# A decoder kernel without its filler transposes of the identity on TensorE

## The chip, the cores and the metric

The kernel runs on one core of one Trainium2 chip. The metric is device time in microseconds (us) of one execution; the values given are medians over runs. Lower is better. TensorE (PE in the profile) does the matrix products, ScalarE (ACT) and VectorE (DVE) the elementwise work and the copies out of the PSUM banks, GpSimd (POOL) some elementwise work, and SyncE (SP) issues the weight transfers. The profile gives TensorE's granted clock as a share of full speed: 1.00 is 2.4 GHz and 0.50 is 1.2 GHz, its two levels.

## The reference

A sequence of 256 rows of width 1024 goes through one block of one kind and four layers of another, in float32:

```python
x = x + 0.5 * _swiglu(_rmsnorm(x, n1_g[l]), ffn1_w_in[l], ffn1_w_out[l])      # d_ff 2816
h = _rmsnorm(x, n2_g[l])
qa, ka, va, qb, kb, vb, qi, ki, wi, ga, gb = jnp.split(h @ w_in[l], split_points, axis=-1)
o_a = _mixer_a(...)      # 8 heads, chunked attention with a relative bias
o_b = _mixer_b(...)      # 8 heads, attention over the 64 keys that 8 index heads select
merged = jax.nn.sigmoid(ga) * (o_a @ w_branch_a[l]) + jax.nn.sigmoid(gb) * (o_b @ w_branch_b[l])
x = x + merged @ w_out[l]
x = x + 0.5 * _swiglu(_rmsnorm(x, n3_g[l]), ffn2_w_in[l], ffn2_w_out[l])
# then, for i in range(4): stick-breaking attention (i = 0, 3), a short convolution (1),
# gated linear attention (2)
m = mixer(rms_norm(h, norm_gains[i, 0])); h = h + rms_norm(m, norm_gains[i, 1])
f = jnp.square(jax.nn.relu(xn @ w_up)) @ w_down; h = h + rms_norm(f, norm_gains[i, 3])   # d_ff 4096
```

## The kernel before

Every product with a weight is made of three products of split operands (high times high, low times high, high times low) so that float32 accuracy is kept at the price of three passes: `split_mm` on lines 1575 to 1577, each of a 128 x 128 tile of the input with 512 columns of the weights. Weights come from memory in parts of 1 MB into four slots; ScalarE makes the high part (`whi`, line 501) and VectorE the low part (`wlo`, line 929). The 256 rows are two tiles of 128.

The program is a fixed list of stages, and each engine has its instructions written out in order; there is no scheduler. Semaphores tie the engines together. The stages are:

- the feed-forward blocks (`ffn`, two gated ones of 11 steps, four squared ones of 8). Their first step is made tile by tile (`job_by_tile`); then `turn(0)` transposes the activated values (line 1654) once `h_ready` says that they exist, and a loop of up, down and turn follows. The last down step stands apart and waits for `hlo_ready`;
- the projections (`lin`) and output projections (`out_layer`, `branch`), which also begin with `job_by_tile`: `turn_y` transposes the normed input of the first row tile (line 1779, eight transposes), ScalarE and VectorE copy it out as `xhi` and `xlo` (VectorE's line 959), the first tile's products run, and after its sixth panel of weights the second row tile is transposed;
- the mixers. `mix_ab` has 8 index scores and then 16 units of scores (lines 1823, 1824), transposes of the probabilities (1851 to 1853) and products with the values (1864, 1865), three to four units in flight; VectorE adds the bias, takes the row's least value and runs a part of the top-64 selection between the first 8 units. `mix_sb` has 16 units (lines 1882, 1883, 1894 to 1896, 1903, 1904) and runs twice. `mix_gla` has 64 small products (line 1963) and then ten groups of products over 64 rows or with a state (lines 1985, 1995, 2001).

Between these stand bursts of `keep_clock(bank, n)`: n transposes of the 128 x 128 identity (line 1569) into columns 384 to 511 of a PSUM bank, columns that nothing reads before they are written again. They wait for nothing of their own. There are 593 in an execution: 16 before `turn(0)` and 16 before the last down step of each feed-forward block, 9 after the first and 4 after the second group of transposes in `job_by_tile`, 16 more ahead of two stages with a long wait (`long_wait`), 4 to 10 at places in the mixers, and 2 at a time inside `mix_ab`'s units.

Of the kernel before, what the change touches and what calls it, by code (L numbers as in the profile page):

```python
# [40 lines left out]
P = 128  # L41
# [25 lines left out]
SPAN = 384  # L67
# [121 lines left out]
def build(nc, x_in, w_parts, gains, const_in, bias_line, conv_w, gla_low, gla_up, gla_b, out):  # L189
    STAGES, TOTAL = stage_list()  # L190

    with ExitStack() as ctx:
# [1367 lines left out]
        def _(pe):  # L1560
            slots = Slots()
            pe.wait_ge(const_sem, 16)

            def keep_clock(bank, n):

                for _ in range(n):
                    nc.tensor.transpose(ps[:, bank, SPAN:SPAN + P], ident, ident)  # L1569

            def split_mm(out_ap, a_hi, a_lo, w_slot, panel, first, last):
# [20 lines left out]
            def job_by_tile(s, banks, slot_ids, n, acc=False, tile_done=None):  # L1592
# [3 lines left out]
                for t in range(NT):  # L1596
                    if turn is not None and t == 0:
                        if s["long_wait"]:
                            keep_clock(6, 16)
                        turn_y(turn, 0)  # L1600
                        keep_clock(6, 9)
                    for j, q in enumerate(slot_ids):
                        if t == 0:
                            pe.wait_ge(lo_ready[q], n[q] + 1)
                        for kk in range(PANELS):
                            k = j * PANELS + kk
                            if turn is not None and k % 4 == 0:
                                pe.wait_ge(xlo_ready, 4 * (s["n_xt"] - 1) + 2 * t + k // 4 + 1)
                            elif k == 0:
                                pe.wait_ge(xlo_ready, 4 * s["n_xt"])  # L1610
                            ins = split_mm(ps[:, banks[t], :], xhi[:, k, t * P:(t + 1) * P], xlo[:, k, t * P:(t + 1) * P],
                                           q, kk, k == 0, k == KT - 1)
                            if turn is not None and t == 0 and k == 5:
                                turn_y(turn, 1)
                                keep_clock(6, 4)
                        if tile_done is not None and t == 0 and j == 1:
                            ins.then_inc(tile_done, 1)
                        if t == NT - 1 and not (acc and j == 1):
                            ins.then_inc(w_used[q], 1)
                    if acc:  # L1620
                        ins.then_inc(acc_ready, 1)
# [16 lines left out]
            def ffn(s, iters, gated):  # L1638
# [21 lines left out]
                job_by_tile(s, (4, 5), (0, 1), {q: slots.take(q) for q in (0, 1)}, tile_done=up_tile0)  # L1660
                keep_clock(6, 16)
                turn(0)
# [18 lines left out]
                n = {q: slots.take(q) for q in dslots}  # L1681
                keep_clock(4, 16)
                for t in range(NT):
# [52 lines left out]
            def out_layer(s, before):  # L1736
                streamed = before in ("mix_conv", "mix_sb")
                first_pairs = 3 if before == "mix_sb" else 1
                if streamed:

                    if before == "mix_conv":
                        keep_clock(6, 10)
                    pe.wait_ge(xlo_ready, 4 * (s["n_xt"] - 1) + first_pairs)
                    job((0, 2), (0, 1), {q: slots.take(q) for q in (0, 1)}, pairs_of=s)
                else:
                    job_by_tile(s, (0, 2), (0, 1), {q: slots.take(q) for q in (0, 1)})
# [61 lines left out]
            def mix_ab(s):  # L1808
# [17 lines left out]
                pe.wait_ge(lin_evac, s["n_lin"])  # L1826
                keep_clock(3, 6)
                for h in range(8):
                    if h >= 4:
                        pe.wait_ge(ix_relu, h - 3)  # L1830
                        keep_clock(3, 2)
                    scores(4 + h % 4, 4 + h // 2, 9, h % 2).then_inc(ix_ready, 1)
                pe.wait_ge(ix_relu, 8)
                keep_clock(3, 8)
                for u in range(20):
# [9 lines left out]
                    if 0 <= v < 16:  # L1845
                        bank = 6 + v % 2
                        if v >= 2:
                            pe.wait_ge(pt_ready, v - 1)
                        keep_clock(bank, 2)
                        pe.wait_ge(p_ready, 2 * v + 2)  # L1850
# [3 lines left out]
                    v = u - 4  # L1854
                    if v < 0:
                        keep_clock(3, 10)
                    if v >= 0:
                        if v < 12:
                            keep_clock(3, 2)
                        pe.wait_ge(pt_ready, v + 1)  # L1860
# [7 lines left out]
            def mix_sb(s):  # L1868
# [4 lines left out]
                pe.wait_ge(lin_evac, s["n_lin"])  # L1873
                keep_clock(3, 4)
                gt, ones = const[:, K_GT:K_GT + P], const[:, K_ONES:K_ONES + P]
                for u in range(20):
                    if u < 16:
                        if u >= 2:
# [5 lines left out]
                                         ).then_inc(z_ready, 1)  # L1884
                        if u < 2:
                            keep_clock(3, 10)
                    v = u - 2
# [66 lines left out]
            def mix_gla(s):  # L1954
# [3 lines left out]
                for h in range(4):  # L1958
                    for n in range(4):
                        for a in range(4):  # L1960
# [3 lines left out]
                                                   GQX[:, c * 64 + 16 * a:c * 64 + 16 * a + 16], start=True, stop=True)  # L1964
                        if n % 2 == 2 - 1:
                            keep_clock(5, 1)
                ins.then_inc(gs_ready, 1)
# [37 lines left out]
                wait_tiles(s, 4)  # L2005
                keep_clock(5, 10)
                pe.wait_ge(kn_sb, 2)
                update(0)
                keep_clock(5, 6)
                pe.wait_ge(gs_sb, 1)  # L2010
# [108 lines left out]
```

## Time and profile before

| | us |
|---|---|
| median of 3 runs | 1928.1 (1928.09 to 1930.03) |
| span of the profiled execution | 1932.3 |
| PE busy | 1886.6 (98%) |
| DVE busy | 1047.2 (54%) |
| ACT busy | 934.6 (48%) |
| POOL busy | 164.0 (8%) |

The profiled execution's span is 4.2 us over the median of the runs. "PE busy" counts every matrix instruction, useful or not, from its start to its modelled end, and neighbours overlap; so the share says that TensorE always has something in hand, not that it runs at its peak. A row of the timeline gives the start, the length, the engine, the line, what is written from what, the shape, how many instructions are merged, and in brackets the idle time of that engine before the first of them and who ended it. A product of float32 operands shows as two instructions.

### The profile page before, as it was taken

To read this page: it belongs to the slowest core of one execution; us is meant where nothing else is said; L and a number is where in the kernel's file an instruction comes from. 1 tells how busy PE (TensorE), PEld (TensorE's weight loads), DVE (VectorE), ACT (ScalarE), POOL (GpSimd) and SP (SyncE) were. 2 spreads that over 40 slices of the span, in tenths; PEclk is the share of its full clock that TensorE was granted. 3 is DMA by queue.
4 is the path that set the end of the run, shared out by engine and by line. 5 is a ranking of instruction groups with operands and counts; after the bars stand their busy time and mean duration, and the time that the engine had idled before them with its cause. 6 is when DMAs were issued, how large, how long until landed. Compare 5 with 4: busy or idle time off the path is not lost.

```text
span 1932.3 us, 23174 instructions
## 1 busy us (share of the span) xinstructions
PE 1886.6 (98%) x9065; PEld 1548.7 (80%) x9065; DVE 1047.2 (54%) x1146; ACT 934.6 (48%) x1103; POOL 164.0 (8%) x150
## 2 busy tenths in 40 slices
PE   7999999999999999999999999999999999999998
PEld 6888887778888787888888888878788888778886
DVE  5555634665555545544467544455754455565443
ACT  5544544645454556444455444355454445655432
POOL 0000010400000013000001000001100100220100
PEclk9999999999999999999999999998999999999999
DMA  7555453034555530544454545452345435224541
GB/s 281 196 181 210 166 213 132 1 140 160 190 186 183 196 131 24 216 174 176 172 202 154 210 174 187 161 196 88 140 172 199 174 141 229 88 98 174 194 154 65
DMA packets 45731, 315.43 MB, mean 163 GB/s; under 512 B 5328, under 2 KB 5456, under 8 KB 9056
## 3 DMA queue, kind: packets, MB, share of 16 engines
q1 hardware_dynamic: 44496, 311.97, 43.2%
q10 hardware_dynamic: 896, 1.49, 0.2%
q0 software_dynamic: 272, 1.05, 0.2%
q8 instruction: 46, 0.75, 0.2%
q14 instruction: 21, 0.17, 0.0%
HBM read 313.44 MB, written 1.05 MB: 163 GB/s over the span
## 4 chain that ended last, share of the span: by engine, by line
PE 89%; DVE 5%; ACT 3%; issue 1%; POOL 1%; DMA 0%; SPq 0%; ACTq 0%; DVEq 0%; POOLq 0%
PE ps L1575 25%; PE ps L1577 25%; PE ps L1576 25%; PE ps L1569 2%; PE ps L1654 2%; DVE wlo L929 1%; PE ps L1882 1%; PE ps L1903 1%; PE ps L1823 1%; DVE xlo L959 1%; PE ps L1779 1%; PE ps L1895 1%; PE ps L1894 1%; ACT whi L501 1%; ACT xhi L672 1%
## 5 line engine op out<-in xcount | busy, mean ns | idle before, releaser
L929 DVE TENSOR_TENSOR wlo<-raw,whi 128x2048 fp32r<-128x2048 f32 x286 | 654.1, 2309 | 443.2 <-ACT whi L501 440.7
L1575 PE MATMUL ps<-whi,xhi 128*128 128x512 f32 x1600 | 630.3, 394 | 6.3 <-DVE xlo L959 5.0
L1577 PE MATMUL ps<-whi,xlo 128*128 128x512 f32 x1600 | 623.4, 390 | 0.0
L1576 PE MATMUL ps<-wlo,xhi 128*128 128x512 f32 x1600 | 622.8, 389 | 0.0
L501 ACT ACTIVATE whi<-raw 128x2048 fp32r<-128x2048 f32 x286 | 538.9, 1911 | 124.0 <-PE ps L1577 110.8
L1575 PEld LDWEIGHTS ps<-whi,xhi 128*128 128x128 f32 x1600 | 300.4, 188 | 70.5 <-issue 7.9
L1577 PEld LDWEIGHTS ps<-whi,xlo 128*128 128x128 f32 x1600 | 300.3, 188 | 63.2
L1576 PEld LDWEIGHTS ps<-wlo,xhi 128*128 128x128 f32 x1600 | 300.6, 188 | 60.1
L1575 PE MATMUL ps<-whi,hhi 128*128 128x512 f32 x688 | 268.7, 391 | 4.1 <-DVE hlo L1118 2.6
L1577 PE MATMUL ps<-whi,hlo 128*128 128x512 f32 x688 | 267.9, 389 | 0.0
L1576 PE MATMUL ps<-wlo,hhi 128*128 128x512 f32 x688 | 267.7, 389 | 0.0
L532 ACT ACTIVATE hhi<-ps 128x1024 fp32r<-128x1024 f32 (+1 forms) x48 | 40.8, 850 | 247.6 <-PE ps L1654 247.3
L1575 PEld LDWEIGHTS ps<-whi,hhi 128*128 128x128 f32 x688 | 129.1, 188 | 32.8 <-DVE wlo L929 3.2
L1577 PEld LDWEIGHTS ps<-whi,hlo 128*128 128x128 f32 x688 | 129.1, 188 | 26.9
L1576 PEld LDWEIGHTS ps<-wlo,hhi 128*128 128x128 f32 x688 | 129.2, 188 | 26.5
L1050 DVE TENSOR_TENSOR hlo<-ps,hhi 128x1024 fp32r<-128x1024 f32 (+1 forms) x48 | 48.1, 1002 | 180.2 <-ACT hhi L532 180.2
L630 ACT ACTIVATE proj<-ps,stat 128x512 f32<-128x512 f32 (+1 forms) x68 | 43.1, 685 | 157.7 <-PE ps L1577 157.7
L1482 POOL TENSOR_TENSOR arena<-arena 128x1024 f32<-128x1024 f32 x28 | 53.1, 1895 | 552.6 <-ACT arena L554 552.6
L1569 PE MATMUL ps<-const 128*128 128x128 f32 x593 | 88.7, 290 | 3.1 <-ACT arena L734 2.3
L554 ACT ACTIVATE arena<-ps,stat 128x512 f32<-128x512 f32 x56 | 35.5, 685 | 109.3 <-PE ps L1577 109.3
L1569 PEld LDWEIGHTS ps<-const 128*128 128x128 f32 x593 | 71.6, 149 | 9.8 <-ACT arena L734 3.0
L1055 DVE SCALAR_TENSOR_TENSOR arena<-ps,stat,arena 128x256 f32<-128x256 f32 x44 | 19.4, 480 | 80.8 <-ACT arena L549 77.9
(212 smaller groups left out, 1277.0 us busy)
## 6 DMA issues: line engine op xcount, KB each, us to landing
raw<-in_w_parts SPq DMA_DIRECT2D x286, 1024.0 KB, 4.9
gain<-in_gains SPq DMA_DIRECT2D x21, 512.0 KB, 4.1
x<-in_x ACTq DMA_DIRECT2D x2, 512.0 KB, 8.8
arena<-in_bias_line POOLq DMA_DIRECT2D x1, 1024.0 KB, 8.3
out<-x SPq DMA_DIRECT2D x2, 512.0 KB, 2.6
const<-in_const_in ACTq DMA_DIRECT2D x1, 320.0 KB, 8.6
wlow<-in_gla_low ACTq DMA_DIRECT2D x1, 64.0 KB, 10.8
wup<-in_gla_up ACTq DMA_DIRECT2D x1, 32.0 KB, 10.3
```

The source lines that it names most:

```text
L501: nc.scalar.activation(whi[s][:], raw[s][:], ACT.Copy).then_inc(hi_ready[s], 1)
L532: nc.scalar.activation(hhi[:, :, 0:kt, :], ps[:, 6:8, 0:kt * P].rearrange("p t (k n) -> p t k n", k=kt), ACT.Copy).then_inc(hhi_ready, 1)
L554: ins = nc.scalar.activation(R[:, t, :], ps[:, 4 + t, :], ACT.Relu, scale=stat[:, RS, ROW_NORM + t:ROW_NORM + t + 1])
L630: ins = nc.scalar.activation(proj[:, t, bass.ds(j * BANK, BANK)], ps[:, 3 + slot + t, :], ACT.Copy, scale=stat[:, RS, ROW_NORM + t:ROW_NOR ...
L929: nc.vector.tensor_tensor(wlo[s][:], raw[s][:], whi[s][:].bitcast(F32), ALU.subtract).then_inc(lo_ready[s], 1)
L1050: nc.vector.tensor_tensor(hlo[:, :, 0:kt, :], ps[:, 6:8, 0:kt * P].rearrange("p t (k n) -> p t k n", k=kt), hhi[:, :, 0:kt, :].bitcast(F32 ...
L1482: nc.gpsimd.tensor_tensor(H[:], R[:], R[:], ALU.mult).then_inc(h_ready, 1)
L1569: nc.tensor.transpose(ps[:, bank, SPAN:SPAN + P], ident, ident)
L1575: nc.tensor.matmul(out_ap, a_hi, wh, start=first, stop=False)
L1576: nc.tensor.matmul(out_ap, a_hi, wl, start=False, stop=False)
L1577: return nc.tensor.matmul(out_ap, a_lo, wh, start=False, stop=last)
L1654: ins = nc.tensor.transpose(ps[:, 6 + t, k * P:(k + 1) * P], H[:, t, k * P:(k + 1) * P], ident)
```

## The change

The helper `keep_clock` and all its calls are gone. Nothing else is edited: no wait, no semaphore and no other instruction is added, removed or moved, on TensorE or on another engine.

```diff
-            def keep_clock(bank, n):
-                for _ in range(n):
-                    nc.tensor.transpose(ps[:, bank, SPAN:SPAN + P], ident, ident)
...
                     if turn is not None and t == 0:
-                        if s["long_wait"]:
-                            keep_clock(6, 16)
                         turn_y(turn, 0)
-                        keep_clock(6, 9)
...
                             if turn is not None and t == 0 and k == 5:
                                 turn_y(turn, 1)
-                                keep_clock(6, 4)
...
                 job_by_tile(s, (4, 5), (0, 1), {q: slots.take(q) for q in (0, 1)}, tile_done=up_tile0)
-                keep_clock(6, 16)
                 turn(0)
...
                 n = {q: slots.take(q) for q in dslots}
-                keep_clock(4, 16)
                 for t in range(NT):
                     if t == 0:
                         pe.wait_ge(hlo_tile0, s["n_ffn"] + 1)
...
-                    if before == "mix_conv":
-                        keep_clock(6, 10)
...
                 pe.wait_ge(lin_evac, s["n_lin"])
-                keep_clock(3, 6)
                 for h in range(8):
                     if h >= 4:
                         pe.wait_ge(ix_relu, h - 3)
-                        keep_clock(3, 2)
                     scores(4 + h % 4, 4 + h // 2, 9, h % 2).then_inc(ix_ready, 1)
                 pe.wait_ge(ix_relu, 8)
-                keep_clock(3, 8)
...
                             pe.wait_ge(pt_ready, v - 1)
-                        keep_clock(bank, 2)
                         pe.wait_ge(p_ready, 2 * v + 2)
...
-                    if v < 0:
-                        keep_clock(3, 10)
                     if v >= 0:
-                        if v < 12:
-                            keep_clock(3, 2)
                         pe.wait_ge(pt_ready, v + 1)
...
-                keep_clock(3, 4)
                 gt, ones = const[:, K_GT:K_GT + P], const[:, K_ONES:K_ONES + P]
...
-                        if u < 2:
-                            keep_clock(3, 10)
...
-                        if n % 2 == 2 - 1:
-                            keep_clock(5, 1)
...
                 wait_tiles(s, 4)
-                keep_clock(5, 10)
                 pe.wait_ge(kn_sb, 2)
                 update(0)
-                keep_clock(5, 6)
                 pe.wait_ge(gs_sb, 1)
```

## Rows read from the trace of the kernel before

**Rows 1.** The page: TensorE's clock in 40 slices, the chain by engine, the fillers' group.

```profile
PEclk9999999999999999999999999998999999999999
...
PE 89%; DVE 5%; ACT 3%; issue 1%; POOL 1%; DMA 0%; SPq 0%; ACTq 0%; DVEq 0%; POOLq 0%
...
L1569 PE MATMUL ps<-const 128*128 128x128 f32 x593 | 88.7, 290 | 3.1 <-ACT arena L734 2.3
```

**Rows 2.** Stretches: length, busy by engine (instructions), granted clock (PEclk), DMA share, GB/s.

```profile
13.20:20.00 6.80, 4.73 (x21) 3.44 (x20) 5.30 (x6) 4.10 (x5) 1.08 (x1) 1.00 0.68 250
326.00:334.00 8.00, 7.35 (x46) 5.57 (x46) 5.04 (x14) 3.86 (x9) 0.00 (x0) 1.00 0.00 0
334.00:347.60 13.60, 13.58 (x50) 11.04 (x50) 8.03 (x36) 2.87 (x12) 2.92 (x4) 0.50 0.01 1
1335.30:1340.90 5.60, 5.60 (x76) 4.58 (x76) 2.27 (x1) 4.86 (x4) 0.70 (x1) 1.00 0.01 3
1341.00:1351.10 10.10, 10.10 (x78) 8.87 (x77) 2.29 (x8) 1.82 (x3) 0.00 (x0) 0.50 0.00 1
1351.20:1370.20 19.00, 19.00 (x90) 11.77 (x88) 9.03 (x17) 7.21 (x13) 5.29 (x1) 1.00 0.00 1
```

**Rows 3.** Timeline of TensorE at the opening of the program.

```profile
9.86 1.97 PE L1779 MATMUL ps<-const,arena 128*128 128x128 f32 x8 [9.86 <-DMA const<-in_const_in]
11.62 1.89 PE L1569 MATMUL ps<-const 128*128 128x128 f32 x9
```

**Rows 4.** Timeline of TensorE at waits inside feed-forward blocks and between stages.

```profile
199.36 1.91 PE L1569 MATMUL ps<-const 128*128 128x128 f32 x16
202.58 0.50 PE L1575 MATMUL ps<-whi,hhi 128*128 128x512 f32 x1 [1.31 <-DVE hlo L1118]
...
412.55 0.47 PE L1575 MATMUL ps<-whi,xhi 128*128 128x512 f32 x1 [1.33 <-DVE xlo L959]
...
633.73 0.66 PE L1779 MATMUL ps<-const,arena 128*128 128x128 f32 x4 [0.89 <-DVE arena L985]
...
793.43 1.91 PE L1569 MATMUL ps<-const 128*128 128x128 f32 x16
796.16 1.09 PE L1654 MATMUL ps<-const,arena 128*128 128x128 f32 x8 [0.81 <-POOL arena L1488]
```

**Rows 5.** Timelines of TensorE and VectorE around a burst of four.

```profile
977.40 0.60 PE L1569 MATMUL ps<-const 128*128 128x128 f32 x4
...
979.24 0.39 PE L1575 MATMUL ps<-whi,xhi 128*128 128x512 f32 x1
...
977.89 1.29 DVE L959 TENSOR_TENSOR xlo<-ps,xhi 128x512 fp32r<-128x512 f32 x2 [1.03 <-ACT xhi L672]
```

**Rows 6.** Timelines of TensorE and VectorE before a squared block's last down step.

```profile
957.43 0.48 PE L1575 MATMUL ps<-whi,hhi 128*128 128x512 f32 x1
...
956.16 1.29 DVE L1118 TENSOR_TENSOR hlo<-ps,hhi 128x512 fp32r<-128x512 f32 x2
```

**Rows 7.** In mix_ab: TensorE's and VectorE's timelines, and the fillers alone in a stretch.

```profile
334.02 1.97 PE L1569 MATMUL ps<-const 128*128 128x128 f32 x8 [0.58 <-ACT proj L743]
335.92 1.22 PE L1823 MATMUL ps<-arena 64*128 64x256 f32 x2
...
347.62 0.70 PE L1823 MATMUL ps<-arena 64*128 64x256 f32 x2
...
337.68 0.42 DVE L1209 SCALAR_TENSOR_TENSOR proj<-ps,arena 128x256 f32<-128x256 f32 x1 [2.40 <-PE ps L1824]
...
353.76 0.42 DVE L1209 SCALAR_TENSOR_TENSOR proj<-ps,arena 128x256 f32<-128x256 f32 x1
...
356.32 0.42 DVE L1209 SCALAR_TENSOR_TENSOR proj<-ps,arena 128x256 f32<-128x256 f32 x1
...
350.26:386.60 36.34, 11.21 (x55) 6.00 (x54) 1.00 0.00 1
```

**Rows 8.** A stretch of the first mix_sb: TensorE's busy time and clock.

```profile
713.70:753.70 40.00, 40.00 (x211) 1.00 0.01 1
```

## The prediction

> **What bounds the kernel now.** I read the page first: TensorE holds 89% of the chain that ended last, so what it does is the time; the other engines matter only where it waits for them [rows 1]. Then the page's clock line: at its best digit in 39 of 40 slices, one less in the other [rows 1]. Then the fillers' group: 593 of them cover 88.7 us of TensorE's time [rows 1]. If the clock did not care, the change could only remove work from the busiest engine. So two questions decide: how much of the 88.7 us lies on the path, and what the clock does without it.
>
> For the second I cut the span where the clock changes. It is at half from 334.0 to 347.6 and from 1341 to 1351.1, and full elsewhere after the opening [rows 2]. What TensorE did before each fall: in the 8 us up to 334 it made transposes and then index scores, products over 64 of its 128 rows with two fillers between, and stood still for the last 0.58 us [rows 2, 7]; from 1335.3 it made the small products of 16 columns [rows 2]. In both it was "busy" nearly all the time, but thinly. It did not fall over 1.33 us of idle time between full transposes, fillers and products [rows 4]. So the thin work of a stretch brings the clock down as well as idle time does, and a filler is work over all rows.
>
> How it rises: in the opening TensorE does nothing but transposes and fillers, from 9.86 us. The nine fillers from 11.62 begin at a pitch of 0.21 us (1.89 us less the last one's length, over eight gaps, gives 0.20 on average) [rows 3], where sixteen at full clock take 1.91 us, a pitch of 0.109 [rows 4]; by 13.2 the clock is full [rows 2]. Only transposes had run by then. The low clock lasted 3.3 us of this work. The Trainium skill says otherwise ("TensorE: Matmul & The Clock Gate", Part 4: PE-mode transpose: full clock does not engage for transpose mode, which does not count as busy in the same way). By that sentence the fillers would hold nothing and the time would be that of the first rival below; the trace disagrees with it.
>
> **What is saved at an unchanged clock.** A filler costs 0.109 us of TensorE's queue [rows 4].
> - Thirteen bursts of four, in `job_by_tile`. After each, six products run and then the second tile's first product needs `xlo`. It starts at 979.24; the first of VectorE's two pieces, which began at 977.89 and take 1.29 us together, is done at about 978.55 [rows 5]. 4 x 0.109 = 0.44 us earlier is 978.80, still behind it. So the whole 0.44 is on the path: 13 x 0.44 = 5.7 us saved. The cover would end at 0.5 us.
> - Four squared blocks' last down step: sixteen fillers end as the product at 957.43 starts without idle time, while VectorE's first `hlo` piece (from 956.16, half of 1.29) is done by 956.85 [rows 6]. 0.45 us each: 1.8 us saved.
> - The other bursts at waits (nine after the first transposes, sixteen before `turn(0)` and before a gated block's last down step) end before what they wait for, with 0.8 to 1.33 us left over [rows 4]. They save nothing; they leave a bare gap.
>
> **What the clock takes back.** I price a fall before dense work like the opening: 3.3 us at half speed [rows 2, 3], of which half, 1.65 us, is lost.
> - Bare gaps in the feed-forward blocks: 796.16 - 793.43 = 2.7 us ahead of `turn(0)` in six blocks, 202.58 - 199.36 = 3.2 us ahead of the last down step in the two gated ones [rows 4]. These eight are twice as long as the idle time that did no harm. The bounds: none falls (0), or all fall and stay low twice as long (8 x 3.3 = 26 us). I take three in four falling, since they are nearer to the two thin stretches than to the harmless 1.33 us, and a quarter of these staying low twice as long, since part of the gap can lie behind the fall: 6 x 1.65 x 1.25 = 12 us.
> - Gaps between stages: ahead of 633.73 one of 0.89 + 1.91 = 2.8 us, then transposes and another gap; a similar pair after `mix_gla`, the other long wait; 1.33 + 1.14 = 2.5 us ahead of 412.55, where nine fillers stood [rows 4]; and the opening, where nine fillers no longer warm the array [rows 3]. In falls of 1.65 I take two, one, three quarters and one: 3.3 + 1.6 + 1.2 + 1.6, less 0.3 for idle time in the opening that covers it, 7.4 us. Bounds 0 and 13. The other gaps between stages are shorter and I take them as harmless.
> - `mix_ab`. It begins earlier: VectorE waited 2.40 us for TensorE ahead of unit 0 [rows 7], and needs 356.32 - 353.76 = 2.56 us per unit after that [rows 7], where bursts of ten at half clock held TensorE for (347.62 - 335.92) / 3 = 3.9 us per unit. Unit 4's scores, at 350.3 before, can follow VectorE's third unit: 337.68 - 2.4 + 2 x 2.56, near 340.4, 10 us earlier. But the clock falls a little sooner than 334 and nothing brings it back: at half clock with fillers, TensorE was busy for 13.6 us and the clock only returned at the end [rows 2], and a unit without fillers is thinner. From unit 4 to the end are 36.1 us, of which 55 fillers x 0.109 = 6.0 [rows 7]. The remaining 30.1 us take 1.8 times as long (a score pair is 0.70 at full and 1.22 at half clock, a filler 0.109 and 0.213 [rows 7]; the gaps between do not double): 54 us. 340.4 + 54 = 394.4 against 386.4, and the last units, denser, warm the array: +7 us. Bounds: -14 if the clock is back by unit 4 (then VectorE and ScalarE set a pace near 2 us), +12.
> - `mix_sb`, twice. The two bursts of ten held unit 2 back; a burst is 1.1 us, and I take 1.0 us as saved. From 713.7 to 753.7 TensorE has no idle time [rows 8], so every product at half clock counts. Without the 24 fillers the clock falls during the first units, where it waits for ScalarE and VectorE. It comes back once units carry both the full-row sums and the value products. I take 12 us at half clock, in which 5.5 us are lost: 2 x (5.5 - 1.0) = 9 us. Bounds: 2 x (-1), and 2 x 34 if all 40 us run at half clock (0.85 of them, as the gaps between products do not double).
> - `mix_gla`. It falls where it fell before, and its fillers go: about 4 us (24 fillers, most at half clock, 0.213 each, less what the wait before the first group takes back). But ten of these fillers were what made the stretch up to 1351.1 dense enough to end the low clock [rows 2]. The 19 us after it are products over 64 rows without idle time [rows 2]; two thirds of them, some 14 us, now run at half clock, until the products over 128 rows with the state come: +12. Net +8; bounds +3 and +13.
>
> Sum: -5.7 - 1.8 + 12 + 7.4 + 7 + 9 + 8 = +36 us. Against the profiled execution that is 1932.3 + 36 = 1968; the median of the runs lies 4.2 lower, so **1964 us**.
>
> **Rivals.**
> - *The fillers hold nothing* (the other side). Then the clock of each stretch is set by the real products, no fall is added, and only work goes: -5.7 - 1.8, `mix_ab` -8 (its late start without a pace at full clock), `mix_sb` -2, `mix_gla` -4, in all -21.5: 1907 us. For it: two falls happened with fillers present [rows 2, 7]. Against it: the opening, and the 1.33 us gap that did no harm with fillers around it. It decides if bare gaps of 2.7 us do not bring the clock down. Chance 0.05. The page of the Trainium skill named above would make it the likeliest.
> - *Short falls.* The gaps cost 12 + 7.4, but the mixers recover at once, so that earlier starts outweigh the low clock there (-5 in all): 1928.1 - 7.5 + 19.4 - 5 = 1935 us. For it: the second fall ended as soon as work was dense. Against: over 13.6 us half filled with fillers it did not. Chance 0.15.
> - *mix_sb stays low*: its 40 us at half clock in both, 2 x 34 in place of 2 x 5.5: 1964 + 57 = 2021 us. For it: nothing in its units is changed between cold and warm. Against: two of three parts of a unit are full-row products. Chance 0.10.
> - *Nothing happens*: losses of the gaps cancel savings, within 0.2% (3.9 us, about what a measurement of this kernel can tell from no change). It needs few falls and quick mixers at once. Chance 0.02.
>
> **How the numbers follow.** My case has 0.68; its own spread, from the bounds on the gaps (half or all falling, +-6) and on the mixers (+-15), is 1945 to 1990. To hold 8 in 10 the range takes that and most of the short falls: 1936 to 1992. Slower 0.93, same 0.02, faster 0.05.
>
> **What the profile after would show.** The granted clock below full in several slices of the page; idle time of 2.7 us ahead of line 1654's product and 3.2 ahead of the gated last down step, and half clock for a few us behind six or so of eight; the second tile's first product 0.44 us nearer to the transposes with no idle time; `mix_ab`'s first VectorE unit some 2 us earlier but its end later than before; `mix_gla`'s groups at half clock; `mix_sb` at half clock for a quarter of its length. I am wrong if the clock stays full behind the bare gaps, or if `mix_ab` is at full clock by its fifth unit.

## The result, and the profile after

| | before | after |
|---|---|---|
| median, us (runs) | 1929.07 (4) | 1968.8 (4), 1967.64 to 1969.62 |
| ratio of the medians | | 1.0202, 95% interval 1.019 to 1.0215 |
| span of the profiled execution, us | 1932.3 | 1967.8 |
| mean granted clock of it | 0.993 | 0.960 |

Without the fillers the kernel is 2.0% slower, 39.7 us. The page of the changed kernel, first TensorE's busy line and then the clock in 40 slices; they answer to [rows 1]:

```profile
PE 1875.0 (95%) x8472; PEld 1515.6 (77%) x8472; DVE 1046.5 (53%) x1146; ACT 934.9 (48%) x1103; POOL 164.7 (8%) x150
...
PEclk9999999599999889999999999998899999899999
```

593 instructions are gone (9065 to 8472), the other engines' busy time is what it was, and six slices now have a clock below the best digit. Lines have other numbers after the change: 1575 to 1577 are 1568 to 1570, 1654 is 1643, 1779 is 1764; a line 1569 in a row of the changed kernel is a product, no filler. The scores of `mix_ab` are on line 1808 there in place of 1823, those of `mix_sb` on 1858 in place of 1882.

The stretches of low clock, and one between them (length, busy by engine, granted clock, DMA share, GB/s), against [rows 2]:

```profile
31.70:35.00 3.30, 3.30 (x10) 2.53 (x9) 3.30 (x3) 2.40 (x2) 0.00 (x0) 0.50 0.79 298
205.80:209.10 3.30, 3.30 (x9) 2.61 (x8) 1.44 (x2) 0.00 (x0) 0.00 (x0) 0.50 0.00 0
335.50:393.40 57.90, 54.32 (x157) 34.22 (x158) 32.33 (x130) 29.07 (x94) 24.06 (x32) 0.50 0.00 0
393.50:424.00 30.50, 27.73 (x128) 21.60 (x127) 19.21 (x18) 15.52 (x12) 0.00 (x0) 1.00 0.36 139
649.50:656.20 6.70, 5.67 (x15) 4.33 (x16) 5.69 (x13) 3.34 (x8) 0.00 (x0) 0.50 0.00 0
728.00:741.60 13.60, 13.01 (x36) 9.76 (x37) 6.01 (x13) 7.11 (x14) 5.33 (x8) 0.50 0.00 1
1362.90:1396.90 34.00, 33.22 (x119) 20.52 (x118) 10.16 (x19) 7.64 (x9) 6.09 (x1) 0.50 0.00 1
1697.40:1714.40 17.00, 17.00 (x49) 12.40 (x48) 6.97 (x14) 8.24 (x16) 5.66 (x9) 0.50 0.00 0
```

The long ones are `mix_ab` (57.9 us), `mix_gla` with what follows it (34.0) and the two `mix_sb` (13.6 and 17.0). The short ones, 3.3 us each, stand behind gaps in the feed-forward blocks. TensorE's timeline at four of these gaps, and at the first tile behind one:

```profile
31.07 0.66 PE L1643 MATMUL ps<-const,arena 128*128 128x128 f32 x4 [2.81 <-DVE arena L1060]
31.48 0.63 PE L1568 MATMUL ps<-whi,xhi 128*128 128x512 f32 x1
31.91 0.63 PE L1569 MATMUL ps<-wlo,xhi 128*128 128x512 f32 x1
...
35.21 0.40 PE L1568 MATMUL ps<-whi,xhi 128*128 128x512 f32 x1
...
204.26 0.50 PE L1568 MATMUL ps<-whi,hhi 128*128 128x512 f32 x1 [3.05 <-DVE hlo L1118]
...
816.66 1.95 PE L1643 MATMUL ps<-const,arena 128*128 128x128 f32 x8 [2.57 <-POOL arena L1488]
...
1446.00 1.09 PE L1643 MATMUL ps<-const,arena 128*128 128x128 f32 x8 [2.57 <-POOL arena L1488]
```

The first gap is bare for 2.81 us, where fillers and 0.9 us of idle time stood. Behind it the products follow each other at 0.43 us (31.48 to 31.91), and from 35.21 on at 0.23. Of two gaps of equal length, 2.57 us, the one at 816.66 is followed by eight transposes in 1.95 us (half clock) and the one at 1446.00 by eight in 1.09 (full clock): the same gap brings the clock down in one place and not in another.

**Where the 35.5 us between the two traces went.** For each place I took the start of the same product in both timelines; the difference of these starts is the lag, and its steps are the losses:

| place | forecast | measured step of the lag |
|---|---|---|
| thirteen bursts of four | -5.7 | -5.5 (0.40 to 0.45 each) |
| last down step of the four squared blocks | -1.8 | -0.5 and then +0.5, each: 0 |
| eight long gaps in the feed-forward blocks | +12 | +10.1: six of eight fell, 1.6 to 1.8 each |
| opening and between stages | +7.4 | +2.9 |
| `mix_ab` | +7 | +7.6 |
| `mix_sb`, twice | +9 | +4.95 and +6.8 |
| `mix_gla` | +8 | +8.3 |
| sum | +36 | +35.2, of 35.5 |

**The profiled execution of before was not a typical one.** The changed kernel's profiled run took 1969.62 us with its span of 1967.8, so 1.8 us lie around a span. The span of before, 1932.3 at a mean clock of 0.993, then belongs to a run of 1934.1, above all runs of the first comparison. Of twelve further runs of before one took 1934.53 us, at a mean clock of 0.993; the others took 1927.98 to 1930.51 at 0.995 or 0.996. (Of 23 more, two took 1937.46 and 1937.51 us at 0.991, the others 1930.39 or less; those two were not profiled.) The fall at 334 us in `mix_ab` [rows 2] is what sets it apart, as the trace without the bursts of four shows below. So against a typical execution the change costs some 6 us more in `mix_ab` than the two traces say. That rests on mean clocks and on traces of other versions; no typical execution of before was itself profiled.

### The profile page after: what moved, and what is told of

Same layout as the page of the kernel before. It is cut to its first block, busy times and chain, and to the rows that moved or that the text cites. A ratio compares the mean times of both kernels' runs of the same rounds, so it can differ in the third digit from the quotient of the medians.

```text
span 1967.8 us, 22002 instructions
## 1 busy us (share of the span) xinstructions
PE 1875.0 (95%) x8472; PEld 1515.6 (77%) x8472; DVE 1046.5 (53%) x1146; ACT 934.9 (48%) x1103; POOL 164.7 (8%) x150
## 3 DMA queue, kind: packets, MB, share of 16 engines
q0 software_dynamic: 272, 1.05, 0.2%
HBM read 313.44 MB, written 1.05 MB: 160 GB/s over the span
## 4 chain that ended last, share of the span: by engine, by line
PE 88%; DVE 6%; ACT 4%; issue 1%; POOL 1%; DMA 0%; SPq 0%; DVEq 0%; ACTq 0%; POOLq 0%
PE ps L1568 25%; PE ps L1570 25%; PE ps L1569 25%; PE ps L1643 2%; DVE wlo L929 2%; PE ps L1858 1%; PE ps L1877 1%; PE ps L1869 1%; DVE xlo L959 1%; PE ps L1868 1%; PE ps L1841 1%; PE ps L1808 1%; ACT whi L501 1%; PE ps L1967 1%; ACT xhi L672 1%
## 5 line engine op out<-in xcount | busy, mean ns | idle before, releaser
L554 ACT ACTIVATE arena<-ps,stat 128x512 f32<-128x512 f32 x56 | 35.5, 684 | 109.4 <-PE ps L1570 109.4
L1643 PE MATMUL ps<-const,arena 128*128 128x128 f32 x344 | 47.8, 278 | 15.9 <-POOL arena L1488 10.3
L1643 PEld LDWEIGHTS ps<-const,arena 128*128 128x128 f32 x344 | 41.1, 142 | 24.6 <-POOL arena L1488 12.0
## 6 DMA issues: line engine op xcount, KB each, us to landing
wup<-in_gla_up ACTq DMA_DIRECT2D x1, 32.0 KB, 10.3
```

The lines of the kernel that those rows point to most:

```text
L554: ins = nc.scalar.activation(R[:, t, :], ps[:, 4 + t, :], ACT.Relu, scale=stat[:, RS, ROW_NORM + t:ROW_NORM + t + 1])
L1643: ins = nc.tensor.transpose(ps[:, 6 + t, k * P:(k + 1) * P], H[:, t, k * P:(k + 1) * P], ident)
```

## Experiments

All runs are compared with the kernel before on the same chip.

### One part alone: the mixers

All `keep_clock` calls in `mix_ab`, `mix_sb` and `mix_gla` removed, those elsewhere kept:

```diff
             def mix_ab(s):
...
-                keep_clock(3, 6)
...
             def mix_sb(s):
...
-                keep_clock(3, 4)
...
             def mix_gla(s):
...
-                keep_clock(5, 10)
```

> The kernel before with the fillers of the three mixers alone removed; those of the feed-forward blocks and between stages stay. Theory (the clock falls in the mixers for want of full-row work, and TensorE sets their pace, so half clock costs time): the lags read in the changed kernel's trace return here, 7.6 us in mix_ab, 11.8 us in the two mix_sb, 7.8 us in mix_gla, in all 27 us: 1929 + 27 = 1956 us, with TensorE's clock at half for some 58 us in mix_ab. Rival (the mixers lose because they enter with a clock that the stages before them have unsettled): with those stages' fillers kept, the mixers recover at once and the earlier starts remain: 1920 to 1930 us.

Measured: 1959.66 us (before 1929.86), ratio 1.0148 (1.0131 to 1.0165): +29.8 us. The stretches of its trace, the mixers' and two others:

```profile
332.90:390.80 57.90, 53.80 (x156) 33.90 (x157) 32.76 (x131) 28.78 (x94) 23.63 (x32) 0.50 0.00 1
...
722.00:732.10 10.10, 10.10 (x30) 7.35 (x30) 4.63 (x10) 5.87 (x12) 3.77 (x6) 0.50 0.01 2
1350.10:1387.40 37.30, 36.52 (x150) 23.39 (x150) 11.95 (x19) 9.92 (x12) 6.09 (x1) 0.50 0.00 1
...
400.00:720.00 320.00, 310.46 (x1469) 256.93 (x1467) 179.57 (x177) 154.88 (x164) 0.00 (x0) 1.00 0.48 179
```

The low stretch of `mix_ab` is 57.9 us again, and between the mixers, where fillers stand, the clock is full. The mixers' loss is their own and not an unsettled clock from before; they are three quarters of the whole (29.8 of 39.7 us). The 27 us had been read against the profiled execution of before. Against that one this trace is 1958.1 - 1932.3 = 25.8 us longer, near the 27; the other 4 us are what that execution (1934.1) lies above the median of 1929.86. The parts moved too: the low stretch of the first `mix_sb` is 10.1 us here and 13.6 in the changed kernel.

### The bursts of four alone

```diff
                                 turn_y(turn, 1)
-                                keep_clock(6, 4)
```

> The kernel before without the thirteen bursts of four alone. Theory (they stand on the path, 0.44 us each, and the clock does not need them): 1929 - 5.7 = 1923.4 us. Rival (the next products then wait for xlo or for weights, as happened behind the last down step of the squared blocks, where 0.5 us was given back within one tile): 1929 us, with new idle time ahead of the second tile's first product.

Measured: 1923.43 us (1923.17 to 1925.38, 7 runs), ratio 0.997 (0.9959 to 0.9981). Its median is 6.4 us below that of before. In its trace each of the thirteen places is passed 0.40 to 0.44 us sooner, 5.4 us in all, and `xlo` and the weights don't take it back. The microsecond between 5.4 and 6.4 is within the spread of the runs (of before: 1927.98 to 1934.53). Its trace also shows `mix_ab` at full clock throughout:

```profile
326.00:390.00 64.00, 63.07 (x370) 48.08 (x369) 42.63 (x146) 43.44 (x110) 24.09 (x32) 1.00 0.07 26
```

The first product after `mix_ab` in its timeline, which starts at 386.40 us in the trace of before:

```profile
379.79 0.50 PE L1575 MATMUL ps<-whi,xhi 128*128 128x512 f32 x1
```

386.40 - 379.79 = 6.6 us, of which 0.43 were there before `mix_ab` began. So 6.2 us of the profiled execution of before are its fall in `mix_ab`, where three bursts of ten at half clock held the units up [rows 7]. Nothing in `mix_ab` differs between the two kernels; whether the clock falls there varies from one execution to the next, as the two mean clocks of before (0.993, and 0.995 or 0.996) say too.

### The sixteens of the feed-forward blocks alone

```diff
-                keep_clock(6, 16)
                 turn(0)
...
-                keep_clock(4, 16)
                 for t in range(NT):
```

> The kernel before without the sixteens inside the feed-forward blocks (ahead of turn(0) and of the last down step), all other fillers kept. Theory (each of the eight long bare gaps has about a three in four chance to bring the clock down, 1.6 us each; the squared blocks' shorter gaps save 0.45 and give it back): +8 to +13 us, 1937 to 1942 us. Rival (a gap of 2.7 to 3.2 us falls only where other fillers nearby are gone too): within 2 us of 1929.

Measured: 1940.12 us (1938.99 to 1952.79, 5 runs), ratio 1.0068 (1.0041 to 1.0094), +10.3 us. In its trace five of the eight gaps are followed by a low stretch; three of the five:

```profile
32.70:35.90 3.20, 3.20 (x9) 2.52 (x8) 3.20 (x3) 2.27 (x2) 0.00 (x0) 0.50 0.74 287
...
630.00:633.20 3.20, 3.20 (x9) 2.46 (x8) 1.52 (x1) 0.00 (x0) 0.00 (x0) 0.50 0.20 82
...
1425.30:1428.60 3.30, 3.30 (x13) 2.92 (x12) 2.61 (x2) 1.60 (x2) 0.00 (x0) 0.50 0.87 318
```

These are not the same gaps as in the changed kernel: the one at 206 and that of the first squared block (816) are spared, and the third squared block's (1425), spared there, falls here. The rival, that a gap falls only where other fillers nearby are gone too, is out. Which gaps fall differs from kernel to kernel, while their number is alike (six and five of eight); what decides it is not shown. The five runs lie far apart, and the longest (1952.79 us at a mean clock of 0.983, where the profiled one had 0.987) was not profiled.

### One burst put back into mix_ab

```diff
                     v = u - 4
+                    if v == 0:
+                        keep_clock(3, 32)
                     if v >= 0:
```

This is the changed kernel with one single burst.

> The changed kernel with one single burst of 32 fillers put back, in mix_ab after unit 4's scores. Theory (nothing in mix_ab's units can raise the clock, but once raised it holds without fillers): the burst takes up to 32 x 0.213 = 6.8 us at half clock, less as the clock rises, and the twelve units after it run at about 2.1 to 2.6 us in place of 3.88: 1968.8 + 5 - 18 = 1956 us, clock full from about 355 us on. Rival (the units themselves are too thin to hold the full clock once the 2-filler bursts are gone): the clock falls again within a few units, 1970 to 1975 us.

Measured: 1953.72 us (1952.09 to 1953.91), ratio to before 1.0121 (1.0106 to 1.0137); 15 us less than the changed kernel. TensorE's timeline at the burst:

```profile
344.42 4.76 PE L1569 MATMUL ps<-const 128*128 128x128 f32 x32
349.10 0.65 PE L1850 MATMUL ps<-proj 128*64 128x256 f32 x2
...
354.36 0.70 PE L1815 MATMUL ps<-arena 64*128 64x256 f32 x2
...
356.71 0.70 PE L1815 MATMUL ps<-arena 64*128 64x256 f32 x2
```

The clock in the stretch from 346.7 us on:

```profile
346.70:380.00 33.30, 30.72 (x168) 20.82 (x167) 21.31 (x79) 24.59 (x78) 19.51 (x26) 1.00 0.00 1
```

In the changed kernel the units follow each other like this:

```profile
348.80 1.22 PE L1808 MATMUL ps<-arena 64*128 64x256 f32 x2
...
352.68 1.22 PE L1808 MATMUL ps<-arena 64*128 64x256 f32 x2
```

3.88 us per unit there, 356.71 - 354.36 = 2.35 here. The clock comes back while 4.8 us of fillers run (they end at 349.18), and the units then hold it without any filler between, up to their end near 381. So `mix_ab`'s loss is not that its units are too thin to keep the full clock; they are too thin to regain it.

### The ten ahead of mix_gla's first state update put back

The changed kernel with `keep_clock(5, 10)` ahead of `pe.wait_ge(kn_sb, 2)` in `mix_gla`.

> The changed kernel with only the ten fillers ahead of mix_gla's first state update put back. Theory (these ten end the low clock before the products over 64 rows, which can't end it themselves): full clock from about 1375 us, 11.5 us of the loss in mix_gla gone, 1.4 us for the burst itself: 1968.8 - 9 = 1960 us. Rival (the low clock there has another cause, or it falls again at once): 1969 to 1971 us.

Measured: 1962.14 us (1960.85 to 1962.9), ratio to before 1.0172; 6.7 us less than the changed kernel. Its stretches:

```profile
1360.70:1370.80 10.10, 10.10 (x73) 9.10 (x74) 2.87 (x9) 3.79 (x5) 0.00 (x0) 0.50 0.01 2
1370.90:1391.20 20.30, 18.49 (x86) 11.15 (x85) 11.43 (x21) 7.71 (x21) 6.17 (x1) 1.00 0.00 1
1391.40:1398.10 6.70, 5.94 (x14) 4.73 (x15) 5.17 (x13) 0.90 (x3) 0.00 (x0) 0.50 0.15 32
```

The low clock ends at 1370.9 in place of 1396.9, and the products over 64 rows keep it. Then it falls once more behind them, in the bare gap of the long wait, where the changed kernel had risen just before: 2.2 us of lag come back there. And the gap of the third squared block, spared in the changed kernel, brings the clock down here (from 1435.7 us) and costs 1.6. So of 10.4 us won in `mix_gla` 10.4 - 2.2 - 1.6 = 6.6 are left in these traces, near the 6.7 of the medians.

### Is it the transpose, or the work?

Four kernels changed what a filler is. First, each filler became a float32 product of the identity with 64 of its columns:

```diff
-                    nc.tensor.transpose(ps[:, bank, SPAN:SPAN + P], ident, ident)
+                    nc.tensor.matmul(ps[:, bank, SPAN:SPAN + 64], ident[0:128, :], ident[0:128, 0:64], start=True, stop=True)
```

> The kernel before with every filler transpose replaced by a float32 product of the identity with 64 of its columns, over all 128 rows, written to the same place. Theory (a filler counts as work over all rows; its being a transpose is beside the point): the clock profile of before, falls only in mix_ab and mix_gla; the time moves by the fillers' own length, some 0.02 us each, so 1925 to 1938 us. Rival (only the transposes hold the clock, or only products do): 1969 us or a clock without any fall.

Measured: 2015.4 us median (2009.13 to 2044.17, 5 runs), ratio 1.0441 (1.0423 to 1.0459), far outside what I expected. I had mis-sized the filler: sixteen of them are 32 instructions and took 3.68 us, where sixteen transposes take 1.91 [rows 4]:

```profile
29.86 3.68 PE L1569 MATMUL ps<-const 128*128 128x64 f32 x32
```

A half of the columns does not make an instruction half as long: 0.11 us each, like one of 128 columns. So this kernel has twice the filler time.

But the clock missed as well as the length. The profiled execution, the longest of the five, has half clock in `mix_ab` for 105.7 us, from 339.8 on, and again in the first `mix_sb` and in `mix_gla`; a part of the first:

```profile
340.00:445.00 105.00, 105.00 (x383) 84.46 (x383) 32.61 (x129) 30.81 (x97) 24.02 (x32) 0.50 0.00 1
```

TensorE has no idle time there, and its fillers go over all rows. The other four runs had mean clocks of 0.970 to 0.975, where before had 0.995 or 0.996. By these an execution of about 2010 us had some 100 to 120 us at half clock, an estimate (twice the missing share of the clock, times the span). So the theory as I wrote it, that work over all rows is what counts, failed here: in `mix_ab` full-row fillers of 64 columns did not hold the clock. In the feed-forward gaps, where they now fill the whole wait, they did; no low stretch lies behind one. The twin over 32 of the 128 rows:

```diff
-                    nc.tensor.transpose(ps[:, bank, SPAN:SPAN + P], ident, ident)
+                    nc.tensor.matmul(ps[:, bank, SPAN:SPAN + 64], ident[0:32, :], ident[0:32, 0:64], start=True, stop=True)
```

> As the run with full rows, the same number of fillers of the same 64 columns, but over 32 of the 128 rows. TensorE is as busy by the profile as there. Theory (what brings the clock down is thin work, and a product over few rows is thin whatever its length): falls in the feed-forward gaps and long low stretches in the mixers as in the changed kernel, and now the fillers' own time on top, doubled where the clock is low: 1970 to 1990 us. Rival (the chip looks at whether TensorE is busy, not at how much of it): the same time and clock as the run with full rows.

Measured: 2122.86 us (2120.4 to 2125.39), ratio 1.1008: 107 us above its twin with the same number of fillers of the same columns, at mean clocks of 0.926 to 0.928 against its 0.970 to 0.975. So rows matter; the size missed, in part for the reason above. The pair was made again with fillers of the right length, one product of 128 columns for two transposes:

```diff
-                for _ in range(n):
-                    nc.tensor.transpose(ps[:, bank, SPAN:SPAN + P], ident, ident)
+                for _ in range((n + 1) // 2):
+                    nc.tensor.matmul(ps[:, bank, SPAN:SPAN + P], ident[0:128, :], ident[0:128, :], start=True, stop=True)
```

> The kernel before with every pair of filler transposes replaced by one float32 product of the identity with its own 128 columns, over all rows (two instructions of 128 columns, as long as two transposes; the runs with 64 columns had fillers of 0.22 us that passed only 64 columns per instruction). Theory (work over all rows is what counts, transpose or product): 1929 us as before, 1926 to 1936, clock falls only in mix_ab and mix_gla. Rival (a transpose counts differently from a product): a clock line with other falls than before, or none.

Measured: 1932.85 us (1932.3 to 1935.48, 10 runs), ratio 1.0016 (1.0007 to 1.0025), 3.3 us more than before. Its trace has half clock in `mix_gla` alone, for 16.9 us in place of 10.1. And the same with `ident[0:32, :]` for both operands:

> The same fillers in number and length over 32 of the 128 rows, so that TensorE is as busy by the profile. Theory (a filler over few rows is thin work, and the clock falls in spite of it): falls in the feed-forward gaps, long low stretches in all three mixers as in the changed kernel, plus the fillers' own time, doubled where the clock is low: 1975 to 2000 us. Rival (busy time counts): the time of the run with full rows, within 5 us.

Measured: 2022.31 us (2021.18 to 2024.07), ratio 1.048 (1.0461 to 1.05). From the page of the run over all rows, TensorE's busy line, the clock and the fillers' group:

```profile
PE 1888.5 (98%) x9086; PEld 1554.6 (80%) x9086; DVE 1046.5 (54%) x1146; ACT 934.5 (48%) x1103; POOL 164.7 (9%) x150
...
PEclk9999999999999999999999999998999999999999
...
L1569 PE MATMUL ps<-const 128*128 128x128 f32 x614 | 91.9, 289 | 3.1 <-ACT arena L734 2.3
```

The same lines of the run over 32 rows:

```profile
PE 1982.7 (98%) x9086; PEld 1606.9 (80%) x9086; DVE 1049.6 (52%) x1146; ACT 934.9 (46%) x1103; POOL 163.3 (8%) x150
...
PEclk9999998579999898999999999998799999799999
...
L1569 PE MATMUL ps<-const 32*128 32x128 f32 x614 | 115.0, 330 | 3.1 <-ACT arena L734 2.3
```

And the stretch of its `mix_ab`:

```profile
335.10:430.50 95.40, 95.11 (x285) 64.62 (x286) 33.62 (x131) 31.91 (x98) 24.10 (x32) 0.50 0.00 1
```

614 fillers in both, TensorE 98% busy in both. Over all rows the clock line is that of before; over 32 rows `mix_ab` runs at half clock for 95.4 us although TensorE is busy for 95.11 of them. That is worse than no fillers at all (2022 against 1969 us): in the mixers the thin fillers cost their time and don't hold the clock. The theory forecast 1975 to 2000 and missed; of the 87 us between the traces, 42 arise in `mix_ab` by the lags, where I had not counted that the units' pairs of fillers are themselves doubled in length for the whole stage.

The theory also had falls in the feed-forward gaps, and there it was wrong. Of the eight gaps one is followed by a low stretch, from 669.6 us; behind the others, two of which lie in the second stretch here, the clock is full:

```profile
669.60:672.80 3.20, 3.20 (x9) 2.50 (x8) 1.90 (x1) 0.00 (x0) 0.00 (x0) 0.50 0.28 118
823.00:1399.00 576.00, 572.27 (x2724) 471.96 (x2722) 315.87 (x300) 270.46 (x284) 46.51 (x22) 1.00 0.48 179
```

So between dense stages thin fillers did hold the clock in seven of eight gaps, where bare gaps lost it in five or six of eight; in the long thin stretches of the mixers they did not. It does not matter within 0.2% whether a filler is a transpose or a product of 128 columns. How many rows it uses matters, and how many columns: with either filler of 128 rows and 128 columns `mix_ab` is at half clock for 13.6 us or not at all, with 128 rows and 64 columns for 106 us, with 32 and 128 for 95, and with 32 and 64 for 126.

### Looking for a better version

Three versions leave out fillers that seemed not to hold anything. The kernel before without the fours and without the pairs in `mix_ab`'s units from unit 4 on:

```diff
-                        keep_clock(bank, 2)
+                        if v < 1:
+                            keep_clock(bank, 2)
...
-                        if v < 12:
-                            keep_clock(3, 2)
```

> The kernel before without the bursts of four and without the pairs of fillers inside mix_ab's units from unit 4 on (the burst ahead of the first transposes stays). Theory (the units hold the full clock once it is there, as the run with one burst showed, and from unit 8 on TensorE sets the pace): -5.7 us, and in mix_ab about nine units x 0.5 = -4 us: 1919 to 1920 us. Rival (VectorE or ScalarE sets the pace of the units, so nothing more is won than without the fours): 1923.4 us. A further one: the clock falls in mix_ab in some executions: above 1930.

Measured: 1921.68 us median of 5, ratio 0.996 (0.9946 to 0.9973), four at 1920.76 to 1922.02 and one at 1929.02. The high one is the profiled one, and it has the fall in `mix_ab`:

```profile
333.70:350.70 17.00, 17.00 (x64) 14.03 (x63) 10.27 (x47) 3.91 (x17) 4.48 (x6) 0.50 0.00 1
```

Of the 4 us forecast for the pairs, 1.7 are left against the 1923.4 without the fours, and the intervals of the two ratios overlap: a gain from the pairs is not shown. Without the fours and the eight single fillers in `mix_gla`:

```diff
-                        if n % 2 == 2 - 1:
-                            keep_clock(5, 1)
```

> The kernel before without the bursts of four and without the eight single fillers between mix_gla's small products. Theory (these eight do not keep the clock there, which falls anyway, and stand on the path): 2.2 us below the run without fours, 1921.2 us. Rival (the low stretch in mix_gla begins earlier or lasts longer without them): 1923.5 us or more.

Measured: 1922.85 us median of 7, 1919.82 to 1934.32, ratio 0.9963 (0.9949 to 0.9978); here too no gain over the version without the fours is shown. And all three edits together:

> As the last one, and the pairs inside mix_ab's units from unit 4 on removed too. Theory: its median adds the 1.7 us that these pairs were worth in the lean run, 1919.5 us, with single executions near 1927 where the clock falls in mix_ab and comes back late. Rival (the pairs' gain was chance): 1921 us.

Measured: 1924.88 us median of 12, ratio 0.998 (0.9953 to 1.0006): six executions at 1918.53 to 1919.38 and six at 1930.38 to 1939.04. The profiled one of these is a high one (1930.38), and so is that of the version before (1934.32). In both it is `mix_gla` that stays low; here the second, then the first:

```profile
1328.80:1362.70 33.90, 33.90 (x125) 22.49 (x126) 13.56 (x19) 6.81 (x5) 4.50 (x1) 0.50 0.00 1
```

```profile
1329.30:1366.70 37.40, 37.40 (x161) 25.54 (x161) 15.55 (x19) 8.89 (x7) 4.50 (x1) 0.50 0.00 1
```

With the single fillers the low stretch lasted 10.1 us in the trace of before [rows 2]. So they seem to hold something, though not what I thought: not the clock during the small products, which falls anyway. In all five traces that have both the single fillers and the ten behind them, over 128 rows and columns, the low stretch lasts 10 to 17 us; in the three that have only the ten it lasts 10 (the run with the ten put back), 34 and 37. Why the ten suffice in one and not in the other two is not shown, nor is it shown that the high executions which were not profiled have the same cause; before itself had two of 23 at 1937.5 us. The version to keep is the one without the fours: 1923.4 us, all seven runs within 2.3 us. It is 0.3% faster than before, and the two single edits on top of it gain nothing that is clear of the noise.

## Why the prediction was right, and where it was off

The forecast was 1964 us, the time 1968.8; it lies in the range and near the likeliest case. That the sum came out at 35.5 us for the +36 is in part luck: between stages and in the gaps 6.4 us too much was forecast, and on the squared blocks, `mix_ab`, `mix_sb` and `mix_gla` some 5.5 us too little.

- **What bounds the kernel.** TensorE sets the time, and the clock decides. Right: of the fillers' 88.7 us [rows 1] only those of the fours, 5.5 us, were won outside the mixers, and the lower clock took more than 35.5 + 5.5 = 41 us.
- **Fours.** Right, alone and within the whole: 5.4 and 5.5 us in the traces for 5.7. The second tile's first product never came to wait for `xlo` or weights; the margin of 0.5 us was not tried, as a burst is 0.44.
- **Squared blocks' last down step.** Wrong. The step "0.45 us each: 1.8 us saved" looked at the wait directly behind the burst and not at the next one. The trace of the changed kernel after the gap:

```profile
979.05 0.50 PE L1568 MATMUL ps<-whi,hhi 128*128 128x512 f32 x1 [0.98 <-DVE hlo L1118]
982.93 0.50 PE L1568 MATMUL ps<-whi,hhi 128*128 128x512 f32 x1 [0.88 <-DVE wlo L929]
```

  The second wait, for `wlo` from VectorE, is 0.88 us. In the trace of before, where the first product stands at 957.43 [rows 6], it was 0.37:

```profile
960.80 0.50 PE L1575 MATMUL ps<-whi,hhi 128*128 128x512 f32 x1 [0.37 <-DVE wlo L929]
```

  VectorE's pace decides there, and 0.5 us of earlier start is given back in full.
- **Long gaps in the feed-forward blocks.** The mechanism and the price were right: three in four falling was forecast, six of eight fell, at 1.6 to 1.8 us each against 1.65. That the number of falls fitted so well is luck: no run shows what decides which gap falls. The factor of 1.25 for staying low twice as long was not needed: every stretch was 3.3 us.
- **Between stages.** Mis-sized: 7.4 forecast, 2.9 measured. The opening lost 0.35 us instead of 1.3, since the low clock passed largely under a wait for weights (before stood still for 0.94 us ahead of 18.55 for `wlo`, and the changed kernel, later by 1.57 us, did not); and the long wait behind `mix_gla` cost nothing in this trace, where the clock had just come back at 1396.9 from `mix_gla`'s own low stretch. In the run with the ten fillers, where it had come back at 1370.9, it fell there for 6.7 us.
- **`mix_ab`.** The size against the profiled execution was right (+7.6 for +7), and so was the stretch at half clock: from unit 4's scores to the first product behind `mix_ab` 53.7 us (343.2 to 396.9) for 54. The bound of -14 us "if the clock is back by unit 4" was too wide: with one burst of 32 the clock was back at 346.7, just behind unit 4's scores, and `mix_ab` took 7.3 us less than in the trace of before; the 15 us are against the changed kernel. With all fillers and full clock throughout it took 6.2 less.
- **`mix_sb`.** 4.95 and 6.8 us for 4.5 each; low for 13.6 and 17.0 us where I had taken 12. The first stretch of half clock begins at 728.0, inside a wait of TensorE for VectorE of 2.70 us, and the two end 2 and 7 us after the first value product. The timeline:

```profile
728.59 1.22 PE L1858 MATMUL ps<-arena 64*128 64x256 f32 x2 [2.70 <-DVE proj L1275]
```

- **`mix_gla`.** Right: +8.3 for +8, and the run with the ten fillers shows that they can end the low clock (at 1370.9 in place of 1396.9). They don't always: it lasted 34 and 37 us in two of the three traces that have them without the single ones.
- **From the trace to the median.** Here is the 5 us that the forecast missed. I took 4.2 us off because the median of before lay so much under the profiled span. But that difference was a fall of the clock in `mix_ab`, which the profiled execution of before had and most others had not, while the changed kernel has one in its trace and, by its mean clocks of 0.960 and 0.961, in all four runs. The sum stood against that execution; it should have stayed there: 1932.3 + 36 = 1968.3 of span, where 1967.8 was measured. This step, "the median of the runs lies 4.2 lower", is the one that failed.
- **Rivals.** "The fillers hold nothing" is out by the first result, and that transposes don't count as work is out by the run with products of the same length: 1929.5 us with transposes, 1932.9 with products, 1968.8 with neither. "Short falls" is out: the mixers stayed low for 13 to 58 us. "`mix_sb` stays low" did not happen.

What stays open: why single gaps of equal length bring the clock down or don't. The traces show that it changes from place to place and from kernel to kernel; no run here controls it. Open too is what a filler needs to hold the clock in the mixers beyond the four kinds tried.

## What to carry to other kernels

Where TensorE waits between bursts of work or makes thin products (few rows, few columns), look at the granted clock of the stretch and not at the busy share; a few microseconds of dense work over all rows and 128 columns, a filler if nothing else is there, at the point before a long thin stretch can be worth three times its own length. A filler that ends before its wait does is free, one that stands on the path must hold the clock somewhere: take such bursts out one kind at a time, and look at all executions, since a version with a better best time can fall onto a second level in half of them. Before adding a sum to a median, ask which execution the trace was and whether its disturbances are in the changed kernel too.

## What the runs showed of the hardware

- A float32 product of 64 columns takes 0.11 us per instruction at full clock, as long as one of 128 columns (3.68 us for 32, against 1.91 for 16 transposes).
- TensorE busy for 95.11 of 95.4 us, with fillers over 32 rows in between, was granted half clock throughout; with the same fillers over 128 rows the clock was full. With fillers over 128 rows but of 64 columns it was at half for 105.7 us, busy without a pause. A busy TensorE is not the same as a full clock.
- Between dense stages even fillers over 32 rows left the clock full behind seven of eight gaps; with the same gaps bare it was full behind two or three of eight.
- The same program has executions on levels apart, with no other change: 1918.5 to 1919.4 and 1930.4 to 1939.0 for one version, at mean clocks of 0.996 or 0.997 and 0.985 to 0.990; in the one that was profiled, of 1930.38 us, the clock came back late in `mix_gla`.
- `mix_ab`'s units keep a clock that they find (full for over 30 us without a filler) and do not regain one that is gone (half for 58 us): what TensorE does at a given moment does not tell its clock; what it did before must be read too.
